# Down products of a mixture-of-experts encoder step in column tiles of 64, 32 and 32

## The chip, the cores and the metric

The kernel runs on one core of a Trainium2 chip. The metric is the device time of one execution in microseconds (us). It is given as the median of several runs of the same program.

## The reference, cut to what matters

The program is one inference step of a two-layer encoder over 256 prompt rows and 32 sample rows, 2048 features wide. Each layer ends in a hierarchical mixture of experts: a router picks one of 4 groups for each row and 2 of the 4 experts in it.

```python
hu = jnp.einsum('td,edf->tef', xt, w_gate_up)      # 2048 -> 1024, for each expert
hg, hv = jnp.split(hu, 2, axis=-1)
act = jax.nn.silu(hg) * hv * gates[..., None]      # 512 wide
out = jnp.einsum('tef,efd->td', act, w_down)       # 512 -> 2048, summed over experts
x = layer_norm(DEEPNORM_ALPHA * x + out, ln_g[i, 1], ln_b[i, 1])
```

The last product is the one that the change touches. All weights are fp32, and each layer has 16 experts of 12 MB each, so the two layers read 403 MB of expert weights.

## The kernel before, in words

Each layer works through its rows in windows, one for each group of experts (further ones would follow if a group overflowed; here there are four windows in each layer). A window holds up to `W = 96` rows ("slots") of one group, and each of its `NE = 4` experts takes up to `ES = 64` of them.

The weights of a window come as 24 chunks of 2 MB through a ring of `NSLOT = 6` slots: 4 chunks of gate and up weights ("gu") and 2 chunks of down weights ("dn") for each expert. SyncE issues them in one order (`WINDOW_ORDER`): gu0, gu1, dn0, gu2, dn1, gu3, dn2, dn3. It waits before each one until TensorE has used up the chunk that was in the slot. TensorE counts that in `parts_used`: a chunk has four parts of 1024 columns, and each part adds one.

A gu part (L1010) is two matmuls of 128 rows by 64 columns of stationary data, one at column tile 0 and one at column tile 64, with 512 moving columns each. They write partitions 0 to 63 and 64 to 127 of one PSUM bank. ScalarE and VectorE make the activations from it (L724, L725, L1522, L1523). TensorE then spreads an expert's 64 rows over the 96 slots of the window (`turn_act`, L969: 64 rows by 128 columns of the array), and ScalarE copies that to `act` (L727).

A dn part (L1023) is two matmuls with 96 slots as the stationary columns and 512 of the 2048 output columns as the moving data. A chunk has two blocks of 128 features (`f`), and each has two parts: the even part writes banks 2 and 3, the odd part banks 4 and 5. The sums of all four experts stay in these four banks over the whole window.

From the third part of dn2's second half on, each part is preceded by a pair of matmuls that picks the rows of the next window (`select_rows`, L944: 96 rows by 128 columns). ScalarE and VectorE take turns to copy them out (L700, L1439).

At the end of a window VectorE adds the four banks to the kept rows (`add_rows`, L1450). It takes the first two banks after the last but one part and the others after the last. Then come the statistics (L1454), a square root by ScalarE (`spread`, L705) and the normalisation. TensorE's first dn part of the next window waits on `z_done` until the four banks are added.

An fp32 matmul of this kernel has two records in the trace, each with its LDWEIGHTS. So L1023 has 1024 records for 512 matmuls, and L1010 has 2048 for 1024.

Of the kernel before, what the change touches and what calls it, by code (L numbers as in the profile page):

```python
# [23 lines left out]
ALU = mybir.AluOpType  # L24
ACT = mybir.ActivationFunctionType
AX = mybir.AxisListType

D = 2048
# [9 lines left out]
NG, NE = 4, 4  # L38
FE = 512
KF = FE // 128  # L40
# [40 lines left out]
OVER_AT = 3  # L81
PLACES_AT = 24
NV = 2 + 2 * NE
OUT_STEP = (16, 32)


# [3 lines left out]
def parts_base(l):  # L90

    return PARTS_LRU + PARTS_OUT + l * NG * PARTS_WIN
# [40 lines left out]
def encoder_step(nc, A, O):  # L133
    ctx = ExitStack()
    with ctx:
# [3 lines left out]
        def sem(name):  # L139
            return ctx.enter_context(nc.semaphore(name))  # L140
# [97 lines left out]
        slot_f = carve(work, 2772, 2, WINS)  # L238
        members = carve(work, 2788, 3, NG + NG * NE)
        rslot = carve(work, 2848, NE)  # L240
        Gh = members[:, :, 0:NG]
        th = carve(arena, 0, FE)
        P = carve(arena, FE, 3, WINS * W)
# [64 lines left out]
        gated = [sem(f"gated{i}") for i in two]  # L308
        sel_ready = [sem(f"sel_ready{i}") for i in two]
        act_ready = [sem(f"act_ready{i}") for i in two]  # L310
        vmoe = [sem(f"vmoe{i}") for i in two]
        x_out = [sem(f"x_out{i}") for i in two]
        P_ready = [sem(f"P_ready{i}") for i in two]
# [42 lines left out]
        def ring_at(n):  # L356
            return ring[:, slot_of(n), :]
# [165 lines left out]
        def _(eng):  # L523
# [140 lines left out]
            def moe(l):  # L664
                if l == 0:
                    eng.wait_ge(brow_in, 64)
                eng.wait_ge(lgT_done[l], 1)
                eng.activation(lgT[:, :], ps[0:20, 1, 0:T], ACT.Identity, bias=brow[:, l:l + 1]).then_inc(lgT_ready[l], 1)

                def rows(i):  # L670
                    t0, m = TILES[i]
                    evacuate_x(1 + l, False, range(4 * i, 4 * i + 4))
                    eng.wait_ge(tr_act[1 + l], 4 * i + 4)
                    eng.dma_start(x_rows[l][t0:t0 + m, :], xtok[0:m, i, :]).then_inc(x_out[l], 16)

                rows(0)
                eng.wait_ge(ex_in[l], 1)
                eng.activation(r4[1][:, :, :], r4[0][:, :, :], ACT.Exp).then_inc(ex_out[l], 1)
                rows(1)
                rows(2)  # L680
                eng.wait_ge(ex_in[l], 2)
                eng.activation(r1[3][:, :, :], r1[2][:, :, :], ACT.Exp).then_inc(ex_out[l], 1)
                if l == 0:

                    eng.wait_ge(cstT_full, 1)
                    eng.activation(cstT[:, :], ps[:, 2, 0:128], ACT.Copy).then_inc(cstT_ready, 1)
                    eng.wait_ge(cstT_ready, 1)
                    dst = [O["lru_conv_prompt"][0, 0, k] for k in range(3)] + [O["lru_conv_sample"][0, 0, k] for k in range(3)]
                    dst += [O["lru_h_prompt"][0, 0], O["lru_h_sample"][0, 0]]
                    for j, o in enumerate(dst):  # L690
                        eng.dma_start(o.rearrange("(b p) -> b p", p=128), cstT[j:128:8, :]).then_inc(out_st, 16)
                else:
                    for i, name in enumerate(("ln_g", "ln_b")):
                        eng.dma_start(ln_row[i], A[name][1, 1:2, :].to_broadcast([W, D])).then_inc(ln_row_in, 16)
                base = C_MOE0 if l == 0 else C_MOE1

                def even_rows(w, q):

                    eng.wait_ge(rows_turned[l], w * PAIRS + (q + 1))
                    eng.activation(xsel[:, 2 * q:2 * q + 2, :], ps[:, 6, :].rearrange("p (k c) -> p k c", k=2), ACT.Copy)\  # L700
                       .then_inc(xsel_even[l], 1)

                def spread(done):
                    eng.wait_ge(zvar_ready[l], done)
                    eng.activation(zr[0:W, :], zr[0:W, :], ACT.Sqrt).then_inc(zstd_ready[l], 1)  # L705

                def normalise(done, done_sem):
                    if l == 0:
                        eng.wait_ge(znorm_ready[l], done)
                        eng.activation(ZS, ZS, ACT.Identity, scale=zr[0:W, :], bias=zn[0:W, :]).then_inc(done_sem, 1)  # L710

                def window(w, first=False):
                    seq = w if l == 0 else w + act_extra[0]

                    parts0 = parts_base(l) + NPART
                    if not first:
                        spread(w)
                        normalise(w, rows_ready[l])
                    eng.wait_ge(act_turned[l], w * (NE + 1) + 1)
                    eng.activation(spread_to[0:ES, :, :], ps[0:ES, 7, 0:NE * W].rearrange("p (e s) -> p e s", e=NE),  # L720
                                   ACT.Copy).then_inc(act_ready[l], 1)
                    for e in range(NE):
                        eng.wait_ge(parts_used, seq * PARTS_WIN + (parts0 + GU_END[e]))
                        eng.activation(th[0:ES, :], ps[0:ES, e % 2, :], ACT.Tanh, scale=0.5)  # L724
                        eng.activation(up[0:ES, :], ps[ES:2 * ES, e % 2, :], ACT.Copy).then_inc(th_ready[l], 1)  # L725
                        eng.wait_ge(act_turned[l], w * (NE + 1) + (e + 2))
                        eng.activation(act[:, e % 2, :], ps[:, 6 + e % 2, 0:KF * W], ACT.Copy).then_inc(act_ready[l], 1)  # L727
                        if e == 1:
                            if not first:
                                eng.wait_ge(rows_out[l], w * OUT_STEP[l])  # L730
                            eng.activation(ZS, XS, ACT.Copy, scale=ALPHA).then_inc(kept[l], 1)
                    for q in range(0, PAIRS, 2):
                        even_rows(w + 1, q)

                for q in range(0, PAIRS, 2):
                    even_rows(0, q)
                for w in range(FLAT):
                    window(w, w == 0)
                eng.wait_ge(route_ready[l], 1)
                n_win = eng.value_load(route_i[0:1, l, 0:1], min_val=NG, max_val=NG + MORE)  # L740
                with eng.Fori(FLAT, n_win) as w:
                    window(w)
                spread(n_win)
                normalise(n_win, rows_last[l])
                if l == 0:
                    act_extra.append(eng.snap(n_win - NG))
                    eng.wait_ge(rows_out[0], eng.snap(n_win * 16))
                    eng.wait_ge(rows_turned[0], eng.snap(n_win * PAIRS + PAIRS))
                    for i, (t0, m) in enumerate(TILES):
                        eng.dma_start(xtok[0:m, i, :], n_rows[t0:t0 + m, :]).then_inc(back_in, 16)  # L750
                    for k in range(0, KD, 2):
                        eng.wait_ge(back_turned, k + 1)
                        g, b = (V_LNG + 1) * KD + k, (V_LNB + 1) * KD + k
                        eng.activation(xT[:, k, :], ps[:, k % 8, 0:T], ACT.Identity, scale=prmT[:, g:g + 1],
                                       bias=prmT[:, b:b + 1]).then_inc(x_ready[1], 1)
# [21 lines left out]
        def _(eng):  # L777
# [122 lines left out]
            def moe(l):  # L900
# [56 lines left out]
                def window(w, first=False):  # L957
# [15 lines left out]
                    for i, (kind, e, q) in enumerate(WINDOW_PARTS):  # L973
# [39 lines left out]
                        else:  # L1013
# [3 lines left out]
                            if e == 0 and q == 0:  # L1017
                                if first:
                                    eng.wait_ge(vgate[l], 2)
                                else:  # L1020
                                    eng.wait_ge(z_done[l], w * 4 + 4)
                            for half in range(2):
                                last = mm(ps[0:W, 2 + 2 * (q % 2) + half, :], act[:, e % 2, f * W:(f + 1) * W],  # L1023
                                          wt[:, half * 512:(half + 1) * 512], start=(e == 0 and f == 0),
                                          stop=(e == NE - 1 and f == KF - 1))
                        last.then_inc(parts_used, 1)

                for w in range(FLAT):
# [55 lines left out]
        def _(eng):  # L1084
# [205 lines left out]
            def moe(l):  # L1290
# [154 lines left out]
                    TT_(sel[0:W, :, :], iota_f[0:W, 0:ES].unsqueeze(1).to_broadcast([W, NE, ES]),  # L1445
                        rslot[0:W, :].unsqueeze(2).to_broadcast([W, NE, ES]), ALU.is_equal).then_inc(sel_ready[l], 1)

                def add_rows(b):
                    zb = ZS[:, b * 512:(b + 1) * 512]
                    TT_(zb, zb, ps[0:W, 2 + b, :], ALU.add).then_inc(z_done[l], 1)  # L1450

                def row_stats(done, b):
                    eng.wait_ge(z_done[l], done * 4 + (b + 1))
# [29 lines left out]
                def window(w, first=False):  # L1483
# [19 lines left out]
                    else:  # L1503
                        fetch_from(w + 1)
                        eng.wait_ge(kept[l], w + 1)
                        for b in range(4):
                            if b % 2 == 0:
                                eng.wait_ge(parts_used, seq * PARTS_WIN + (parts_base(l) + NPART + (-1 if b == 0 else 0)))
                            add_rows(b)
                        for b in range(4):  # L1510
                            row_stats(w, b)
                        row_var(w)
# [50 lines left out]
                for b in range(4):  # L1563
                    if b % 2 == 0:
                        eng.wait_ge(parts_used, eng.snap((n_win + extra) * PARTS_WIN + (parts_base(l) + NPART - (b == 0))))
                    add_rows(b)
                    row_stats(n_win, b)
                row_var(n_win)
                row_scale(n_win)
# [82 lines left out]
```

## Time and profile before

| | us |
|---|---|
| median of 3 runs (lowest to highest) | 1631.03 (1627.22 to 1642.02) |
| the profiled execution | 1641.09 |
| its span | 1639.3 |
| TensorE busy with matmuls | 1533.7 |
| VectorE busy | 498.0 |
| ScalarE busy | 366.4 |

The span runs from the first to the last instruction of the profiled execution. The mean granted TensorE clock in it was 0.962 of full speed. Busy times of different engines overlap.

### The profile page before, as it was taken

The page shows a single profiled execution, that of the slowest core. Times are in us where ns is not written, and L with a number is a line of the kernel's source. Part 1 is how long each engine was busy: PE and PEld are TensorE (multiplying, and loading weights), DVE is VectorE, ACT ScalarE, POOL GpSimd, SP SyncE. Part 2 cuts the span into 40 slices and gives each one's busy share as a digit, 9 for nine tenths or more (in the row PEclk, how much of TensorE's full clock was granted, in tenths as well). Part 3 has the DMA queues.
Part 4 walks back from the last instruction along what each step waited for, and adds up shares of the span by engine and source line. Part 5 has one row for each costly group of instructions (what it writes and reads, how often), then busy time and mean ns, then how long its engine had stood idle before and what let it go on. Part 6 is the DMA issues. An engine that isn't in the chain of part 4 may idle for free.

```text
span 1639.3 us, 16481 instructions
## 1 busy us (share of the span) xinstructions
PE 1533.7 (94%) x6944; PEld 881.7 (54%) x6944; DVE 498.0 (30%) x1046; ACT 366.4 (22%) x554; POOL 22.1 (1%) x34
## 2 busy tenths in 40 slices
PE   4999997999899999999999968979999999999995
PEld 4999996997643433443443435654344344344333
DVE  4676767554430020020020027533003003003003
ACT  3556566333300021021021011230101101101100
POOL 0000000000000000000000000000000000000000
PEclk8999998999889999999999987978999999999998
DMA  9445554542289989999999962337998999999990
GB/s 301 141 158 166 167 167 156 182 176 103 79 344 396 406 351 395 428 412 401 428 412 403 420 233 82 130 116 315 392 426 332 395 428 401 396 428 406 404 408 16
DMA packets 89045, 487.77 MB, mean 298 GB/s; under 512 B 5324, under 2 KB 59276, under 8 KB 61356
## 3 DMA queue, kind: packets, MB, share of 16 engines
q1 hardware_dynamic: 83984, 463.75, 71.6%
q0 software_dynamic: 2464, 13.37, 2.7%
q10 hardware_dynamic: 2522, 9.59, 1.8%
q8 instruction: 55, 0.90, 0.2%
q14 instruction: 20, 0.16, 0.0%
HBM read 476.15 MB, written 14.47 MB: 299 GB/s over the span
## 4 chain that ended last, share of the span: by engine, by line
PE 75%; DMA 18%; DVE 4%; ACT 1%; issue 1%; ACTq 0%; DVEq 0%; POOL 0%; POOLq 0%
PE ps L1023 22%; PE ps L1010 18%; DMA ring<-in_moe_w_down 15%; PE ps L944 5%; PE ps L840 4%; PE ps L842 4%; PE ps L841 4%; PE ps L870 2%; PE ps L872 2%; PE ps L871 2%; PE ps L1073 2%; PE ps L852 2%; PE ps L969 1%; DMA xtok<-x_rows,src_now 1%; PE ps L878 1%
## 5 line engine op out<-in xcount | busy, mean ns | idle before, releaser
L1023 PE MATMUL ps<-ring,work 128*96 128x512 f32 x1024 | 461.6, 596 | 8.1 <-DMA ring<-in_moe_w_down 8.1
L1010 PE MATMUL ps<-ring,xsel 128*64 128x512 f32 x2048 | 457.3, 602 | 1.5 <-DMA ring<-in_moe_w_gate_up 1.4
L1010 PEld LDWEIGHTS ps<-ring,xsel 128*64 128x64 f32 x2048 | 144.3, 138 | 293.7 <-issue 285.9
L1023 PEld LDWEIGHTS ps<-ring,work 128*96 128x96 f32 x1024 | 164.2, 164 | 247.0 <-issue 228.8
L1522 DVE SCALAR_TENSOR_TENSOR arena<-arena,ps 64x512 f32<-64x512 f32 x32 | 21.7, 679 | 604.5 <-ACT work L725 604.5
L840 PE MATMUL ps<-operands,whi 128*128 128x288 f32 x512 | 154.5, 302 | 9.1 <-ACT mark L597 9.1
L842 PE MATMUL ps<-operands,ring_lo 128*128 128x288 f32 x512 | 152.4, 298 | 0.0
L841 PE MATMUL ps<-ring_lo,whi 128*128 128x288 f32 x512 | 151.7, 296 | 0.0
L1153 DVE TENSOR_TENSOR ring_lo<-ring,whi 128x1024 fp32r<-128x1024 f32 x96 | 116.1, 1223 | 80.0 <-ACT whi L586 79.7
L586 ACT ACTIVATE whi<-ring 128x1024 fp32r<-128x1024 f32 x96 | 100.9, 1058 | 156.6 <-PE ps L842 97.5
L944 PEld LDWEIGHTS ps<-work,xtok 96*128 96x128 f32 x320 | 87.2, 319 | 39.9 <-issue 17.0
L724 ACT ACTIVATE arena<-ps 64x512 f32<-64x512 f32 x32 | 18.9, 590 | 396.2 <-PE ps L1010 396.1
L1439 DVE COPY xsel<-ps 128x512 f32<-128x512 f32 x40 | 27.7, 691 | 248.4 <-PE ps L944 248.4
L840 PEld LDWEIGHTS ps<-operands,whi 128*128 128x128 f32 x512 | 97.1, 190 | 9.6 <-issue 9.2
L944 PE MATMUL ps<-work,xtok 96*128 96x256 f32 x320 | 90.1, 414 | 11.6 <-DMA xtok<-x_rows,src_now 11.6
L841 PEld LDWEIGHTS ps<-ring_lo,whi 128*128 128x128 f32 x512 | 97.0, 189 | 0.4
L842 PEld LDWEIGHTS ps<-operands,ring_lo 128*128 128x128 f32 x512 | 97.0, 189 | 0.0
L870 PE MATMUL ps<-operands,whi 128*128 128x288 f32 x256 | 76.9, 300 | 12.2 <-DVE ylo L1247 12.2
L872 PE MATMUL ps<-operands,ring_lo 128*128 128x288 f32 x256 | 76.4, 298 | 0.0
L871 PE MATMUL ps<-ylo,whi 128*128 128x288 f32 x256 | 76.1, 297 | 0.0
L700 ACT ACTIVATE xsel<-ps 128x512 f32<-128x512 f32 x40 | 23.9, 597 | 181.2 <-PE ps L944 181.2
L727 ACT ACTIVATE work<-ps 128x384 f32<-128x384 f32 x32 | 15.7, 490 | 205.7 <-PE ps L969 205.7
(295 smaller groups left out, 1179.3 us busy)
## 6 DMA issues: line engine op xcount, KB each, us to landing
ring<-in_moe_w_gate_up SPq DMA_DIRECT2D x128, 2048.0 KB, 16.3
ring<-in_moe_w_down SPq DMA_DIRECT2D x64, 2048.0 KB, 19.0
ring<-in_lru_w_in SPq DMA_DIRECT2D x16, 2048.0 KB, 9.6
ring<-in_lru_w_out SPq DMA_DIRECT2D x8, 2048.0 KB, 8.8
x_rows<-xtok ACTq DMA_DIRECT2D x4, 1024.0 KB, 3.9
ring<-in_pool_w SPq DMA_DIRECT2D x4, 1024.0 KB, 18.3
xtok<-in_x_prompt SPq DMA_DIRECT2D x2, 1024.0 KB, 9.0
ring<-in_lru_w_a SPq DMA_DIRECT2D x8, 256.0 KB, 5.4
```

What stands on the lines that cost most here:

```text
L586: eng.activation(whi[:, p % NPART, :], ring_at(n)[:, at * PART:(at + 1) * PART], ACT.Copy)\
L840: mm(o, hi, yhi[:, k, :], start=(k == 0), stop=False)
L841: mm(o, hi, xlo_block(k), start=False, stop=False)
L842: last = mm(o, lo, yhi[:, k, :], start=False, stop=(k == KD - 1))
L852: last = mm(ps[:, 4 + 2 * a + b, 0:TG], wv[:, a, k, b * 128:(b + 1) * 128], UC[:, k, :], start=(k == 0), stop=(k == 1))
L870: mm(o, hi, yhi[:, k, :], start=(k == 0), stop=False)
L871: mm(o, hi, ylo[:, k, :], start=False, stop=False)
L872: last = mm(o, lo, yhi[:, k, :], start=False, stop=(k == KD - 1))
L944: last = mm(ps[:, 6 + q % 2, b * 256:(b + 1) * 256], XS.rearrange("s (c p j) -> s c j p", c=4, j=4)[:, k // 4, k % 4, :], sel[0:W, :, :].r ...
L1010: last = mm(ps[half * ES:(half + 1) * ES, e % 2, :], xsel[:, k, e * ES:(e + 1) * ES], wt[:, half * 512:(half + 1) * 512], start=(k == 0), ...
L1023: last = mm(ps[0:W, 2 + 2 * (q % 2) + half, :], act[:, e % 2, f * W:(f + 1) * W], wt[:, half * 512:(half + 1) * 512], start=(e == 0 and f ...
L1153: TT_(lo_at(n, at), ring_at(n)[:, at * PART:(at + 1) * PART], whi[:, p % NPART, :].bitcast(F32), ALU.subtract).then_inc(lo_ready, 1)
```

## The change

Each group of two full-width dn products per part becomes column-tiled products over three banks. Bank 2+r (r = 0, 1, 2) gets three matmuls that have different columns of the array: slots 0 to 63 of output block r in column tile 0 (64 wide), slots 64 to 95 of block r in the tile at column 64 (32 wide), and 32 slots of output block 3 in the tile at column 96 (32 wide). Which 32 slots of block 3 a bank holds is given by `LAST_OF_BANK`. The even part does banks 2 and 3, the odd part bank 4, and bank 5 isn't used. ScalarE copies block 3 from partitions 96 to 127 of the three banks to `last_block` in three copies, and VectorE adds block 3 from there, after a wait on `last_ready`.

```diff
+QB = 32
+LAST_OF_BANK = (2, 0, 1)
...
+                def take_last():
+
+                    for r, c in enumerate(LAST_OF_BANK):
+                        last = eng.activation(last_block[c * QB:(c + 1) * QB, :], ps[3 * QB:4 * QB, 2 + r, :], ACT.Copy)
+                    last.then_inc(last_ready[l], 1)
+
...
                     if not first:
+                        eng.wait_ge(parts_used, seq * PARTS_WIN + parts0)
+                        take_last()
                         spread(w)
                         normalise(w, rows_ready[l])
...
+                extra = 0 if l == 0 else act_extra[0]
+                eng.wait_ge(parts_used, eng.snap((n_win + extra) * PARTS_WIN + (parts_base(l) + NPART)))
+                take_last()
                 spread(n_win)
                 normalise(n_win, rows_last[l])
...
-                            for half in range(2):
-                                last = mm(ps[0:W, 2 + 2 * (q % 2) + half, :], act[:, e % 2, f * W:(f + 1) * W],
-                                          wt[:, half * 512:(half + 1) * 512], start=(e == 0 and f == 0),
-                                          stop=(e == NE - 1 and f == KF - 1))
+                            wt = ring_at(n)[:, (f % 2) * D:(f % 2 + 1) * D]
+                            start, stop = e == 0 and f == 0, e == NE - 1 and f == KF - 1
+                            for r in ((0, 1), (2,))[q % 2]:
+                                c = LAST_OF_BANK[r]
+                                for rows, slots0, d in ((0, 0, r), (2 * QB, 2 * QB, r), (3 * QB, c * QB, 3)):
+                                    m = 2 * QB if rows == 0 else QB
+                                    last = mm(ps[rows:rows + m, 2 + r, :], act[:, e % 2, f * W + slots0:f * W + slots0 + m],
+                                              wt[:, d * 512:(d + 1) * 512], start=start, stop=stop, tile_position=(0, rows))
                         last.then_inc(parts_used, 1)
...
-                def add_rows(b):
+                def add_rows(b, done):
                     zb = ZS[:, b * 512:(b + 1) * 512]
-                    TT_(zb, zb, ps[0:W, 2 + b, :], ALU.add).then_inc(z_done[l], 1)
+                    if b == 3:
+                        eng.wait_ge(last_ready[l], done)
+                    TT_(zb, zb, ps[0:W, 2 + b, :] if b < 3 else last_block[0:W, :], ALU.add).then_inc(z_done[l], 1)
```

## Rows read from the trace of the kernel before

**Rows 1.** The page: busy time by engine, and the clock and DMA in 40 slices.

```profile
PE 1533.7 (94%) x6944; PEld 881.7 (54%) x6944; DVE 498.0 (30%) x1046; ACT 366.4 (22%) x554; POOL 22.1 (1%) x34
...
PEclk8999998999889999999999987978999999999998
DMA  9445554542289989999999962337998999999990
```

**Rows 2.** The page's costliest groups: busy us, mean ns of one, idle before.

```profile
L1023 PE MATMUL ps<-ring,work 128*96 128x512 f32 x1024 | 461.6, 596 | 8.1 <-DMA ring<-in_moe_w_down 8.1
L1010 PE MATMUL ps<-ring,xsel 128*64 128x512 f32 x2048 | 457.3, 602 | 1.5 <-DMA ring<-in_moe_w_gate_up 1.4
```

**Rows 3.** Two windows behind the first, layer 0: busy by engine, PEclk, DMA share, GB/s.

```profile
598.65:724.20 125.55, 124.08 (x455) 50.66 (x456) 14.99 (x31) 16.22 (x22) 1.84 (x2) 1.00 1.00 412
724.20:849.77 125.57, 124.22 (x455) 50.65 (x456) 15.15 (x31) 16.22 (x22) 1.84 (x2) 1.00 1.00 414
```

**Rows 4.** DMA issues: count, KB each, median us to landing.

```profile
ring<-in_moe_w_gate_up SPq DMA_DIRECT2D x128, 2048.0 KB, 16.3
ring<-in_moe_w_down SPq DMA_DIRECT2D x64, 2048.0 KB, 19.0
```

**Rows 5.** The timeline of TensorE's matmuls in window 1, layer 0: start, us, what.

```profile
604.99 8.80 PE L1010 MATMUL ps<-ring,xsel 128*64 128x512 f32 x40
613.73 7.11 PE L1023 MATMUL ps<-ring,work 128*96 128x512 f32 x16
620.77 1.18 PE L969 MATMUL ps<-work,arena 64*128 64x96 f32 x8
621.87 7.11 PE L1023 MATMUL ps<-ring,work 128*96 128x512 f32 x16
628.91 14.02 PE L1010 MATMUL ps<-ring,xsel 128*64 128x512 f32 x64
```

**Rows 6.** The timeline of weight loads there: start, us, what, idle before.

```profile
598.58 0.20 PEld L1010 LDWEIGHTS ps<-ring,xsel 128*64 128x64 f32 x4
...
599.07 0.14 PEld L1010 LDWEIGHTS ps<-ring,xsel 128*64 128x64 f32 x2 [0.29 <-issue]
599.50 0.14 PEld L1010 LDWEIGHTS ps<-ring,xsel 128*64 128x64 f32 x2 [0.29 <-issue]
...
619.39 0.16 PEld L1023 LDWEIGHTS ps<-ring,work 128*96 128x96 f32 x1 [0.27 <-issue]
619.82 0.16 PEld L1023 LDWEIGHTS ps<-ring,work 128*96 128x96 f32 x1 [0.27 <-issue]
620.76 1.01 PEld L969 LDWEIGHTS ps<-work,arena 64*128 64x128 f32 x8 [0.78 <-issue]
```

**Rows 7.** The line L1010 by itself: ns min/median/max of a record.

```profile
L1010 PE MATMUL ps<-ring,xsel x2048: 592/592/1112, 448.1 to 1582.8; 128*64 128x512 f32 x187
```

**Rows 8.** The timeline of matmuls where the next window's rows are picked.

```profile
681.69 3.67 PE L1023 MATMUL ps<-ring,work 128*96 128x512 f32 x8
685.21 1.08 PE L944 MATMUL ps<-work,xtok 96*128 96x256 f32 x4
686.12 1.88 PE L1023 MATMUL ps<-ring,work 128*96 128x512 f32 x4
687.84 1.08 PE L944 MATMUL ps<-work,xtok 96*128 96x256 f32 x4
```

**Rows 9.** Stretches late in the first window of layer 0; columns as in rows 3.

```profile
570.00:575.00 5.00, 5.00 (x16) 3.08 (x16) 0.69 (x1) 0.60 (x1) 0.00 (x0) 1.00 0.41 170
575.00:580.00 5.00, 5.00 (x17) 3.29 (x16) 0.77 (x2) 1.88 (x2) 0.00 (x0) 1.00 0.70 223
580.00:585.00 5.00, 5.00 (x15) 1.68 (x15) 2.41 (x6) 0.00 (x0) 0.00 (x0) 1.00 0.48 200
585.00:590.00 5.00, 5.00 (x26) 1.70 (x24) 3.80 (x12) 1.05 (x2) 0.00 (x0) 1.00 0.93 326
```

**Rows 10.** The last window of layer 1: its last dn chunks, and the final adds.

```profile
1584.51 7.10 PE L1023 MATMUL ps<-ring,work 128*96 128x512 f32 x16 [1.07 <-DMA ring<-in_moe_w_down]
...
1615.51 5.31 PE L1023 MATMUL ps<-ring,work 128*96 128x512 f32 x12
...
1619.14 0.68 DVE L1450 TENSOR_TENSOR xtok<-xtok,ps 96x512 f32<-96x512 f32 x1 [2.63 <-PE ps L1023]
...
1623.10 0.67 DVE L1450 TENSOR_TENSOR xtok<-xtok,ps 96x512 f32<-96x512 f32 x1
```

**Rows 11.** ScalarE's copy of 64 partitions by 512 columns out of PSUM.

```profile
L725 ACT ACTIVATE work<-ps 64x512 f32<-64x512 f32 x32 | 19.0, 593 | 0.4
```

More of the change, by code:

```diff
@@ L240, in encoder_step @@
         rslot = carve(work, 2848, NE)
+        last_block = carve(work, 3584, 512)
         Gh = members[:, :, 0:NG]
@@ L310, in encoder_step @@
         act_ready = [sem(f"act_ready{i}") for i in two]
+        last_ready = [sem(f"last_ready{i}") for i in two]
         vmoe = [sem(f"vmoe{i}") for i in two]
@@ L1508, in window @@
                                 eng.wait_ge(parts_used, seq * PARTS_WIN + (parts_base(l) + NPART + (-1 if b == 0 else 0)))
-                            add_rows(b)
+                            add_rows(b, w)
                         for b in range(4):
@@ L1565, in moe @@
                         eng.wait_ge(parts_used, eng.snap((n_win + extra) * PARTS_WIN + (parts_base(l) + NPART - (b == 0))))
-                    add_rows(b)
+                    add_rows(b, n_win)
                     row_stats(n_win, b)
```

## The prediction

> **What bounds the kernel now.** I read the busy times first [rows 1]: TensorE is busy for 94% of the span, and in the slices of the expert windows (11 to 22 and 27 to 38) both it and the DMA engines stand at 8 or 9 tenths. The costliest groups [rows 2] are the two products of the experts: 461.6 us of down products (L1023) and 457.3 us of gate and up products (L1010). The windows view by window [rows 3] decides what a saving on TensorE can be worth. A window takes 125.6 us, TensorE is busy for 124.1 to 124.2 of them, and the DMA share is 1.00 at 412 to 414 GB/s. So the two are level. The issues view says the same: a chunk of 2 MB lands 16 to 19 us after its issue [rows 4], while 24 chunks in 125.6 us are one in 5.2 us. Some three chunks are thus always queued. TensorE waits for the ring only 9.5 us in all [rows 2] because it is just about as slow as the loads. VectorE and ScalarE are idle for over two thirds of the span.
>
> **How matmuls follow each other.** The change stands or falls with this, so I read the timeline for it. In a run of equal shapes a new record starts every 0.43 us: the weight loads of L1023 stand 0.43 us apart [rows 6], and 16 records end 7.11 us after the first starts [rows 5], which is 15 x 0.43 plus the 0.59 of the last one. In the gate and up products the loads come in pairs every 0.43 us [rows 6], and 40 records take 8.80 us [rows 5], which is 19 x 0.43 + 0.59 with some slack. So two tiles of 64 columns run at the same time, and equal tiles are known to be concurrent here.
>
> Where the shape of the tile changes it is different. L1010's 40 records begin at 604.99 and end at 613.79, and L1023 begins at 613.73, with the records' length of 0.59 [rows 5, 7] and not their spacing of 0.43 between the last start and the next. The 16 records of L1023 end at 620.84, and L969 (64 rows by 128 columns) begins at 620.77; those of the next chunk end at 628.98, and L1010 begins at 628.91 [rows 5]. The weight load in front isn't started early either: 0.78 us pass without a load, against 0.27 inside a run [rows 6]. Each of these changes of tile shape thus lets the array run empty. The two that I can compare cost 0.59 - 0.43 = 0.16 us, and then the first spacing is 0.49 (598.58 to 599.07 [rows 6]) in place of 0.43.
>
> The Trainium skill says of this (TensorEngine Tiling (Array Packing), section Tiling Modes) that changing the tiling mode, and not just the tile, drains TensorE, and it lists 128x64 and 128x32 as different modes. The rows above agree with the drain for 64 against 128 columns; none shows 64 beside 32.
>
> **The change part by part.**
>
> *The products.* Before, a block f has 4 matmuls, that is 8 records; a chunk has two blocks, 16 records, and takes 7.04 us (613.73 to 620.77 [rows 5]). After, a block has 3 banks with 3 matmuls each, 18 records. No row shows a 64-column tile beside 32-column ones, so the cost of a bank has two ends.
> - Lower end: all three tiles run together as the pairs of L1010 do. A bank takes 2 x 0.43 = 0.86 us and a chunk 6 x 0.86 = 5.15. That is 1.9 us less than now, or 1.7 without the drain at the end of the chunk.
> - Upper end: the 64-column tile and each 32-column tile drain each other. A tile alone takes 0.49 + 0.59 = 1.08 us, a bank 3.24, a chunk 19.4.
> - Between them: 64 and 32 columns are different shapes, but the two 32-column tiles are equal and run together. A bank takes 1.08 for the first and 1.08 for the pair, 2.16 us, and a chunk 6 x 2.16 = 12.96 us.
>
> I take the third. The rows that are nearest to a change from 64 to 32 columns are the changes from 64 to 128 and from 128 by 128 to 64 by 128, and each of them drained, also where the new tile begins at the same corner as the old. Then a chunk costs 12.96 - 7.04 = 5.92 us more, and 64 chunks 379 us.
>
> *What TensorE no longer waits for.* At 24 x 5.2 us the loads are far ahead of a window that takes 170 us, so the ring waits of 9.5 us go [rows 2].
>
> *The picks of the next rows.* A pick and a part take 2.63 us together (685.21 to 687.84) and a part 1.72 (686.12 to 687.84), so a pick is 0.91 us now, with no drain since both are 128 wide [rows 8]. After, it follows and precedes other shapes: it keeps its last record's full 0.40 (1.08 us for four records less three spacings of 0.22) in place of 0.22, and the first spacing grows by 0.06. That is about 0.2 us for each of 64, or 13 us.
>
> *ScalarE's three copies.* Each moves 32 by 512; the nearest row is 64 by 512 at 0.59 us [rows 11], so 1.8 us after a window's last part. They are hidden: VectorE's adds and statistics of blocks 0 to 2 fill some 4 us, as now (1619.14 to 1623.10 [rows 10]), before it wants block 3. Queued behind the new wait on ScalarE are `spread` and `normalise`, which need VectorE's later results anyway, and then the copy for the next window's activations, some 14 us of TensorE work away. I take nothing. Without that cover it would be 1.8 us at each of the two layer ends.
>
> *The last adds.* The final part is one bank. VectorE starts on blocks 0 and 1 that long before the end (2.16 us against 1.7), and its work of eight steps ends about when it did. In the lower case the bank is 0.86 us, and each layer ends 0.9 us later against TensorE.
>
> *Sum.* 379 - 9.5 + 13 = +382 us on the profiled execution of 1641, so 2023. The median of the runs shown stands 10 us below that execution, which gives 2013.
>
> **The rivals.**
>
> *A. All three tiles run together: faster.* For it speaks that tiles of different columns do run together in L1010, and that every drain in the rows is between shapes that overlap in the array, which 64, 32 and 32 don't. TensorE's window would fall by 8 chunks x 1.7 = 14 us to 110. But the loads fill all of 125.6 us in the windows behind the first [rows 3], so there the 14 us become ring waits. What is left is the time in which the DMA engines are idle now: in the first window of a layer their share is 0.41, 0.70, 0.48 and 0.93 between 570 and 590 [rows 9], which is 7.4 us idle, and I take as much for layer 1. And the end of a layer: the last ring wait is before dn2, at 1584.5 [rows 10], and the four chunks behind it save 4 x 1.7 = 6.9 us. That is 14.3 us for a layer, 29 for both, less 2 for the later adds; a few us may come from packing the loads tighter. 27 to 36 us less gives 1641 - 30 = 1611, and 1601 against the median.
>
> *B. The tiles run together only in part: slower by a little.* If records start in the program's order and the second record of a tile holds back the next tile, three tiles need three spacings, 1.29 us for a bank and 3.86 for a block, against 3.43 now. That is 0.43 x 16 = 6.9 us more in a window, of which 1.5 are today's wait: +5.4 x 8 = 43 us, 1675. Against it speaks that the pairs of L1010 start together from their first record on (four loads within 0.20 us, and 2 for each spacing [rows 6]).
>
> *C. All three drain each other.* By the upper end a chunk costs 12.4 us more, +790, so 2430.
>
> The other side of my forecast is A. It decides at the cost of a bank: below 4/3 x 0.86 = 1.14 us the change saves TensorE time, and above it the kernel is slower, since the loads leave only 1.5 us in a window.
>
> **How the numbers follow.** Drain between 64 and 32: 0.54. A: 0.36, of which 0.03 fall within 1%, since the loads could leave less than I count. B: 0.06. C: 0.04. So faster by over 1% is 0.33, within 1% is 0.03, slower is 0.64; 1% is about what a measurement of this kernel can tell from no change. The likeliest case is the drain, 2013 us. Its own range comes from the spacing after a drain (0.43 or 0.51 in place of 0.49) and the picks: 1965 to 2045. The range has to reach A at 1590 to leave out no more than 2 in 10, and takes in B; it ends at 2050.
>
> **What would show each step.** Drain: L1023's busy time rises from 461.6 to about 830 us, the records stand 0.4 to 0.6 us apart one by one in the 64-column tile and in pairs behind it, the ring waits vanish, the DMA share in a window drops from 1.00 to about 0.75, and a window takes 170 us. A: three records start within some ns of each other every 0.43 us, L1023 is busy about 345 us, and TensorE gets waits on the down and gate loads of over 10 us a window at a DMA share of 1.00. B: a chunk takes 7.7 us. ScalarE's copies are right if no wait of VectorE on them is longer than a few tenths. The prediction is wrong if the array takes tiles of unequal width at the same time; everything else in the sum is small beside that.

## The result, and the profile after

The changed kernel takes 1955.5 us (median of 4 runs, 1946.1 to 1958.4) against 1633.1 for the kernel before. The ratio is 1.196, with a 95% interval from 1.193 to 1.200. The profiled execution has a span of 1956.6 us, 317 us more than before.

The page of the changed kernel, its busy times, clock and DMA in 40 slices, to be read against [rows 1]:

```profile
PE 1861.6 (95%) x8224; PEld 849.3 (43%) x8224; DVE 498.6 (25%) x1046; ACT 380.4 (19%) x578; POOL 22.1 (1%) x34
...
PEclk8999989998999999999999969899999999999998
DMA  8555554426883985896598234387769839858930
```

TensorE is as busy as ever, at 95%, but the DMA row has lost most of its nines in the expert windows. VectorE's 498.6 us are those of before, and ScalarE has 14 us more for 24 copies. So whatever grew is on TensorE. The groups of the changed kernel with different shapes kept apart (busy us, mean ns of one):

```profile
L1025 PE MATMUL ps<-ring,xsel 128*64 128x512 f32 x2048 | 455.1, 600 | 0.0
L1043 PE MATMUL ps<-ring,work 128*64 128x512 f32 x768 | 410.5, 616 | 0.0
L1043 PE MATMUL ps<-ring,work 128*32 128x512 f32 x1536 | 404.0, 605 | 0.0
```

The down products are now L1043. They took 461.6 us [rows 2]; now their 64-column tiles alone are busy for 410.5 us and the 32-column tiles for 404.0. If the two kinds ran side by side these two numbers would be the same stretch of time. The page has 768.8 us for both together. That is 45.7 less than their sum of 814.5, or 0.06 for each of the 768 turns of a width. That is about how far the row of a turn's last matmul runs on past the start of the next shape, and no overlap of the work. The ring waits behind both products are gone.

The weight loads in the changed kernel's window 1, layer 0, show the pattern (start us, us, what, idle before):

```profile
657.42 0.14 PEld L1043 LDWEIGHTS ps<-ring,work 128*32 128x32 f32 x4 [0.81 <-issue]
658.41 0.19 PEld L1043 LDWEIGHTS ps<-ring,work 128*64 128x64 f32 x2 [0.84 <-issue]
659.41 0.14 PEld L1043 LDWEIGHTS ps<-ring,work 128*32 128x32 f32 x4 [0.81 <-issue]
660.39 0.19 PEld L1043 LDWEIGHTS ps<-ring,work 128*64 128x64 f32 x2 [0.84 <-issue]
```

Two loads of 64 columns, then four of 32, then two of 64, each group about a microsecond after the other, with 0.81 to 0.84 us in which nothing is loaded. That gap is the mark of a change of tile shape that [rows 6] had too (0.78, against 0.27 to 0.29 inside a run). The tile of 64 columns has the array to itself for 1.00 us (658.41 to 659.41), then the two of 32 have it for 0.98 (659.41 to 660.39). A bank takes 1.98 us.

The timeline of the same stretch gives the chunk, and a stretch of layer 1's last window gives the picks; both in the changed kernel:

```profile
656.47 11.93 PE L1043 MATMUL ps<-ring,work 128*64 128x512 f32 x36
668.33 1.18 PE L984 MATMUL ps<-work,arena 64*128 64x96 f32 x8
669.44 11.98 PE L1043 MATMUL ps<-ring,work 128*64 128x512 f32 x36
681.35 9.23 PE L1025 MATMUL ps<-ring,xsel 128*64 128x512 f32 x42
...
1907.04 1.30 PE L959 MATMUL ps<-work,xtok 96*128 96x256 f32 x4
1908.27 4.04 PE L1043 MATMUL ps<-ring,work 128*64 128x512 f32 x12
```

A chunk takes 11.86 to 11.91 us (656.47 to 668.33, 669.44 to 681.35) where it took 7.04 [rows 5], and a pick 1.23 (1907.04 to 1908.27) where it took 0.91 [rows 8]. That accounts for the result: 64 x 4.85 = 310 us, 64 x 0.32 = 21, less the ring waits of 9.5, is 321 us, beside the 317 by which the span grew.

Two windows of the changed kernel (busy by engine, clock, DMA share, GB/s), and the times from issue to landing:

```profile
641.43:806.72 165.29, 165.29 (x614) 46.71 (x613) 15.09 (x31) 17.99 (x25) 1.84 (x2) 1.00 0.79 315
806.72:972.01 165.29, 165.29 (x613) 46.70 (x613) 15.24 (x31) 17.99 (x25) 1.84 (x2) 1.00 0.78 314
...
ring<-in_moe_w_gate_up SPq DMA_DIRECT2D x128, 2048.0 KB, 12.1
ring<-in_moe_w_down SPq DMA_DIRECT2D x64, 2048.0 KB, 10.6
```

A window is 165.3 us instead of 125.6 [rows 3]. TensorE has no idle time in it, and the loads use 0.79 of the DMA engines and land after 11 to 12 us instead of 16 to 19 [rows 4]: the two are no longer level.

### The profile page after: what moved, and what is told of

The parts are those of the page before. It is cut to its first block, busy times and chain, and to the rows that moved or that the text cites. A ratio compares the mean times of both kernels' runs of the same rounds, so it can differ in the third digit from the quotient of the medians.

```text
span 1956.6 us, 19069 instructions
## 1 busy us (share of the span) xinstructions
PE 1861.6 (95%) x8224; PEld 849.3 (43%) x8224; DVE 498.6 (25%) x1046; ACT 380.4 (19%) x578; POOL 22.1 (1%) x34
## 4 chain that ended last, share of the span: by engine, by line
PE 92%; DVE 3%; DMA 2%; ACT 1%; issue 1%; ACTq 0%; DVEq 0%; POOL 0%; POOLq 0%
PE ps L1043 39%; PE ps L1025 23%; PE ps L959 5%; PE ps L855 4%; PE ps L857 4%; PE ps L856 3%; PE ps L984 2%; PE ps L885 2%; PE ps L887 2%; PE ps L886 2%; PE ps L1092 2%; PE ps L867 1%; DMA xtok<-x_rows,src_now 1%; PE ps L893 1%; PE ps L1066 1%
## 5 line engine op out<-in xcount | busy, mean ns | idle before, releaser
L1043 PE MATMUL ps<-ring,work 128*32 128x512 f32 (+1 forms) x2304 | 768.8, 608 | 0.0
L1043 PEld LDWEIGHTS ps<-ring,work 128*32 128x32 f32 (+1 forms) x2304 | 130.6, 117 | 570.4 <-issue 568.1
L959 PE MATMUL ps<-work,xtok 96*128 96x256 f32 x320 | 104.9, 460 | 12.3 <-DMA xtok<-x_rows,src_now 12.3
L959 PEld LDWEIGHTS ps<-work,xtok 96*128 96x128 f32 x320 | 82.5, 325 | 69.7 <-issue 53.7
## 6 DMA issues: line engine op xcount, KB each, us to landing
ring<-in_moe_w_gate_up SPq DMA_DIRECT2D x128, 2048.0 KB, 12.1
```

The costliest lines, as they stand in the source:

```text
L959: last = mm(ps[:, 6 + q % 2, b * 256:(b + 1) * 256], XS.rearrange("s (c p j) -> s c j p", c=4, j=4)[:, k // 4, k % 4, :], sel[0:W, :, :].r ...
L1043: last = mm(ps[rows:rows + m, 2 + r, :], act[:, e % 2, f * W + slots0:f * W + slots0 + m], wt[:, d * 512:(d + 1) * 512], start=start, stop ...
```

## The experiments

Theory W: a change between 64 and 32 columns empties the array, and equal tiles run together however many they are. Rival N: the array runs at most two of these fp32 tiles at a time, whatever their widths.

**Four tiles of 32** (e1_four_of_32). Nothing but the widths is changed.

```diff
-for rows, slots0, d in ((0, 0, r), (2 * QB, 2 * QB, r), (3 * QB, c * QB, 3)):
-    m = 2 * QB if rows == 0 else QB
+for rows, slots0, d in ((0, 0, r), (QB, QB, r), (2 * QB, 2 * QB, r), (3 * QB, c * QB, 3)):
+    m = QB
```

Expected: 

> All down products in four column tiles of 32: slots 0 to 31, 32 to 63 and 64 to 95 of block r, and block 3 at column 96; everything else as in the changed kernel. Theory W (a change between 64 and 32 columns empties the array; equal tiles run together however many they are): a bank takes 2 x 0.43 = 0.86 us instead of 1.98, a chunk 5.15 us, the loads become the bound, and the time is about 1600 us (1590 to 1615). Rival N (the array runs at most two of these fp32 tiles at a time, whatever their widths): a bank takes at least 4 x 0.43 = 1.72 us, a chunk 10.3, and the time is about 1633 + 64 x 3.3 = 1840 us.

Measured: 1606.5 us, 0.985 of the kernel before (0.980 to 0.989). That is 349 us less than the changed kernel, with a third more matmuls in the down products. The weight loads of this kernel, in the same place of the window:

```profile
601.24 0.16 PEld L1043 LDWEIGHTS ps<-ring,work 128*32 128x32 f32 x8 [0.81 <-issue]
601.70 0.13 PEld L1043 LDWEIGHTS ps<-ring,work 128*32 128x32 f32 x4 [0.30 <-issue]
602.12 0.13 PEld L1043 LDWEIGHTS ps<-ring,work 128*32 128x32 f32 x4 [0.30 <-issue]
602.55 0.13 PEld L1043 LDWEIGHTS ps<-ring,work 128*32 128x32 f32 x4 [0.30 <-issue]
```

Four loads every 0.43 us: four tiles run at once, and the only long gap is the one in front, where the 64-column tiles of the gate and up products end. N is out. This version is faster than the kernel before too, by 1.5%.

**Widths grouped** (e2_widths_grouped). The same matmuls as in the changed kernel, in an order with fewer changes.

```diff
-for r in ((0, 1), (2,))[q % 2]:
-    for rows, slots0, d in ((0, 0, r), (2 * QB, 2 * QB, r), (3 * QB, c * QB, 3)):
+banks = ((0, 1), (2,))[q % 2]
+wide = [(r, 0, 0, r) for r in banks]
+narrow = [t for r in banks for t in ((r, 2 * QB, 2 * QB, r), (r, 3 * QB, LAST_OF_BANK[r] * QB, 3))]
+for r, rows, slots0, d in wide + narrow:
```

Expected: 

> The changed kernel with the even part's matmuls in another order: first the 64-column tiles of banks 2 and 3, then the four 32-column tiles of both; two changes of width in that part instead of four. Theory W: the four records of 64 columns take 0.48 + 0.43 + 0.43 + 0.52 = 1.86 us and the four pairs of 32 columns 1.84, together 3.70 us against 3.97 now; 0.27 us for each of 128 even parts are 35 us, so about 1920 us. Rival N (at most two tiles at a time, no matter the widths): the order changes nothing that the width did, about 1955 us.

Measured: 1921.0 us, 1.176 of before (1.172 to 1.180). The median is 34.5 us below the changed kernel's and the span of the profiled execution, 1917.9 us, is 38.7 below. There are 256 changes of width less, so one costs 0.13 to 0.15 us. The rest of the loss stays, since the 64-column tiles still have the array alone. The weight loads of an even part show it:

```profile
653.22 0.19 PEld L1044 LDWEIGHTS ps<-ring,work 128*64 128x64 f32 x2 [0.84 <-issue]
...
655.08 0.14 PEld L1044 LDWEIGHTS ps<-ring,work 128*32 128x32 f32 x4 [0.81 <-issue]
...
656.92 0.19 PEld L1044 LDWEIGHTS ps<-ring,work 128*64 128x64 f32 x2 [0.84 <-issue]
```

The two 64-column tiles take 1.86 us one after the other (653.22 to 655.08), and the four of 32 columns, in pairs, 1.84 (655.08 to 656.92).

**Without the fourth tile, and with a second tile of 64** (e3_no_fourth_tile, e6_two_of_64). Each leaves part of the down products out or misplaced. The two differ in the width of one tile (the first keeps the fourth tile for one of a window's 16 blocks).

```diff
 # e3
+    if rows == 3 * QB and not start:
+        continue
-    ... start=start, stop=stop, tile_position=(0, rows))
+    ... start=start, stop=stop or rows == 3 * QB, tile_position=(0, rows))
 # e6
-for rows, slots0, d in ((0, 0, r), (2 * QB, 2 * QB, r), (3 * QB, c * QB, 3)):
-    m = 2 * QB if rows == 0 else QB
+for rows, slots0, d in ((0, 0, r), (2 * QB, QB, r)):
+    m = 2 * QB
```

Expected of the first: 

> The changed kernel with the tile at column 96 issued only for the first block of a window, so that output block 3 misses the other 15 blocks; what runs is one tile of 64 columns and one of 32 for each bank. Theory W: the two still take turns, a bank stays at 1.98 us, and the time is within 1% of 1956 us. Rival N: two tiles run together, a bank takes 0.86 us, and the time falls to about 1600 us.

Expected of the second: 

> As the run without the fourth tile, but the second tile is 64 columns wide as well: slots 32 to 95 at column 64, so that rows 64 to 95 hold other slots' sums and block 3 is no product. Only the width of the second tile differs from that run, and three banks are used. Theory W: equal widths run together, 0.86 us for a bank and about 1600 us. Rival N gives the same here. A third reading, that a second tile in the down products waits for another reason (the part's counting, the order of the two records of a matmul), gives about 1950 us.

Measured: 1953.0 and 1610.4 us, one execution each. The shapes of the down products in the first run (two rows), then in the second (one row):

```profile
L1045 PE MATMUL ps<-ring,work 128*64 128x512 f32 x768 | 410.5, 616 | 0.0
L1045 PE MATMUL ps<-ring,work 128*32 128x512 f32 x816 | 401.6, 605 | 0.0
```

```profile
L1043 PE MATMUL ps<-ring,work 128*64 128x512 f32 x1536 | 353.6, 599 | 11.3 <-DMA ring<-in_moe_w_down 11.3
```

With nearly half of the 32-column matmuls left out (816 records in place of 1536), those tiles are still busy for 401.6 us, since a tile of 32 columns by itself takes as long as two. Two tiles are enough for the loss, and 32 more columns in one of them take it away. It is the width, not the number of tiles, the column at which they begin, or the order of a matmul's two records. No run puts 32 columns into a tile of 64, so a tile's width and the number of columns it uses are not told apart for these two. For full-width tiles [rows 8] tell them apart: products with 96 stationary columns and picks with 128 follow each other there at the full pace of 0.43 us.

**Three blocks at full width** (e4_three_blocks_wide). No tiles at all; this asks what a saving of a quarter of the down products is worth.

```diff
-for half in range(2):
+for half in range(2 if q % 2 == 0 or (e == 0 and f == 0) else 1):
...
-    ... stop=(e == NE - 1 and f == KF - 1))
+    ... stop=(e == NE - 1 and f == KF - 1) or (q % 2 == 1 and half == 1))
```

Expected: 

> The kernel before, but the fourth output block (bank 5) is multiplied only for the first of a window's 16 blocks of features, so that 15 of its 16 contributions are missing. TensorE's down work falls to three quarters with no tiles and no changes of width at all. Reading 'the loads are the bound' (rival A's account): the windows behind the first stay near 124.5 us with ring waits of 6 to 8 us each, and only the first windows and the ends of the layers get shorter; 1595 to 1612 us, as with four tiles of 32. Rival reading (four tiles of 32 lose something of their own, above all in the changes of shape around the picked rows): this run is clearly faster than four tiles of 32, 1575 to 1590 us.

Measured: 1601.5 us, 0.979 of before (0.977 to 0.982). So four tiles of 32 give up little against nearly the same saving without tiles: 5 us by the medians, and 9 by the ratios of 0.985 and 0.979, which were taken on different chips. Where TensorE waits in this run, then in the one with four tiles of 32 (us in total, times, longest):

```profile
PE ps L1010 <- DMA ring<-in_moe_w_gate_up: 44.2, 22, 5.3
PE ps L1023 <- DMA ring<-in_moe_w_down: 17.8, 17, 1.4
```

```profile
PE ps L1025 <- DMA ring<-in_moe_w_gate_up: 37.0, 19, 5.6
PE ps L1043 <- DMA ring<-in_moe_w_down: 10.2, 9, 1.3
```

In this run the down products are busy for 103 us less (358.5 in place of 461.6). Of that, 52 us come back as waits for the weights (62.0 in place of 9.5) and 13 in slower gate and up products (470.3 in place of 457.3); the span is 38 us shorter. With four tiles of 32 it is 109 us less (352.8), of which 38 come back as waits, 12 in the gate and up products and 12 in the picks (102.2 in place of 90.1); the span is 37 us shorter, and about 10 are not accounted for by these rows.

So the reading that four tiles of 32 lose something of their own around the picked rows is true in part. In the first window of layer 0 of that run, eight picks and the seven parts between them take 20.3 us (547.91 to 568.19), and 19.3 in the kernel before (559.66 to 579.00): there the tiles save nothing. The window takes 124.2 us with four tiles of 32 (447.60 to 571.76) and 121.6 in this run (448.52 to 570.09). In the windows behind it the weights are waited for either way.

**Half of the down loads** (e7_four_of_32_half_dn_loads, e8_before_half_dn_loads), on four tiles of 32 and on the kernel before.

```diff
+if kind == "dn":
+    src, dst = src[:, 0:SLOT // 2], dst[:, 0:SLOT // 2]
```

The second half of each down chunk then holds older data.

Expected of the first: 

> The run with four tiles of 32, with only the first half of each down chunk loaded, so that the second half holds older data; the same instructions otherwise. The loads of a window fall from 24 chunks to 20. If the loads are what bounds that run, its ring waits (47 us in all) go for the most part and the time falls by 35 to 50 us, to about 1560 us. If something on TensorE or the copies behind it bounds it, the time stays within 1% of 1606 us.

Expected of the second: 

> The kernel before with only the first half of each down chunk loaded, so that the second half holds older data. TensorE is level with the loads there: its ring waits are 9.5 us. Theory: those waits go and nothing else changes, 1618 to 1626 us. Rival (loads and products also slow each other down, by memory traffic or by late slots): 1600 us or less.

Measured: 1543.6 and 1624.3 us, one execution each. So the loads do bound the version with four tiles of 32; it gains more than I expected, 60 us of span (1602.3 to 1541.9). Its waits of 47 us explain the larger part. The rest is in the gate and up products, which are busy for 469.6 us with the waits and 455.9 without them. The reason is the clock. Four stretches of 5 us of the version with four tiles of 32, around its ring wait of 3.2 us (columns as in [rows 3]):

```profile
618.00:623.00 5.00, 2.01 (x10) 0.43 (x6) 0.00 (x0) 0.00 (x0) 0.00 (x0) 0.93 0.99 298
623.00:628.00 5.00, 4.77 (x12) 1.49 (x14) 0.00 (x0) 0.00 (x0) 0.00 (x0) 0.50 1.01 429
628.00:633.00 5.00, 5.00 (x22) 1.36 (x18) 0.00 (x0) 0.00 (x0) 0.00 (x0) 0.89 1.02 436
633.00:638.00 5.00, 5.00 (x50) 1.46 (x48) 1.36 (x2) 1.19 (x2) 0.00 (x0) 1.00 1.02 436
```

After the stretch in which TensorE was busy for 2.01 of 5 us, the granted clock is 0.50 for the next one, that is 1.2 instead of 2.4 GHz, and the products run at half their pace until it is back. The timeline of TensorE there shows what it costs, and that it doesn't follow every wait:

```profile
623.23 10.01 PE L1025 MATMUL ps<-ring,xsel 128*64 128x512 f32 x32 [3.21 <-DMA ring<-in_moe_w_gate_up]
...
644.85 7.09 PE L1025 MATMUL ps<-ring,xsel 128*64 128x512 f32 x32
...
657.38 3.65 PE L1025 MATMUL ps<-ring,xsel 128*64 128x512 f32 x16 [1.25 <-DMA ring<-in_moe_w_gate_up]
```

Behind the wait of 3.21 us, 32 records take 10.01 us in place of 7.09; behind one of 1.25 us, 16 records take the usual 3.65. The whole run has five ring waits of 3.2 to 5.6 us. The 32 records behind them take 10.01, 8.78, 10.01, 8.80 and 9.94 us, 12.1 us more than five times 7.09, which is nearly all of the 13.7. The other ring waits, of 2.2 us at most, are followed by records at the usual pace. A long ring wait is thus dearer than its own length, and a short one isn't.

On the kernel before, 1624.3 us lies in the range that I gave for the case that only its waits go. It is 10 us under the median of 1634.5 measured beside it, and the waits are 9.5. (Against the span of the profiled execution it is 17, but that execution was 8 us above its median.)

**The copies alone** (e5_copies_alone). The full-width products of before, with block 3 taken out of bank 5 by ScalarE.

```diff
-last = eng.activation(last_block[c * QB:(c + 1) * QB, :], ps[3 * QB:4 * QB, 2 + r, :], ACT.Copy)
+last = eng.activation(last_block[c * QB:(c + 1) * QB, :], ps[c * QB:(c + 1) * QB, 5, :], ACT.Copy)
```

Expected: 

> The products of the kernel before (96 slots, four banks) with the change's other half: ScalarE copies output block 3 out of bank 5 in three copies of 32 partitions, and VectorE adds it from there after the wait on ScalarE. Theory: the copies are hidden behind VectorE's first adds, no change, within 0.3% of before. Rival: the copies and the load of the square root's table behind them lie on the path at the end of each window, at least 1.8 us at each layer's end, and the next window's activations wait too: 1637 to 1650 us.

Measured: 1634.8 us, 1.000 of before (0.998 to 1.001). The copies cost nothing that can be measured.

**Pairs of 64, then four of 32** (e9_pairs_of_64_then_32s). A forecast from theory W: both widths may be used if they take few turns and each fills the array. All products are made, but some lie where the adds don't look for them.

```diff
-for r in ((0, 1), (2,))[q % 2]:
-    for rows, slots0, d in ((0, 0, r), (2 * QB, 2 * QB, r), (3 * QB, c * QB, 3)):
+if q % 2 == 0:
+    tiles = [(b, half * ES, ES, 0, 2 * b + half) for b in range(2) for half in range(2)]
+else:
+    tiles = [(2, c * QB, QB, 2 * QB, c) for c in range(4)]
+for r, rows, m, slots0, d in tiles:
```

Expected: 

> Both widths in use, but never side by side: the even part multiplies slots 0 to 63 of all four output blocks as two pairs of 64-column tiles (banks 2 and 3), the odd part slots 64 to 95 of the four blocks as four 32-column tiles in bank 4. All products are made, but lie where the adds that follow don't look for them, so the sums that reach the rows are mixed up. Two changes of width for each block of features, against six in the changed kernel. Theory W (the price is one of each change, about 0.15 us, and of what a lone tile leaves unused): the even part takes 0.48 + 0.43 + 0.43 + 0.52 = 1.86 us, the odd part 0.45 + 0.53 = 0.98, a chunk 5.7 us; that is 0.4 us more than four tiles of 32 and under the loads' pace, so 1604 to 1614 us, faster than before. Rival (mixing widths costs by itself, whatever the order): a chunk of over 8 us and a time above 1660 us.

Measured: 1610.0 us, 0.987 of before (0.985 to 0.990). A chunk (32 records) in its timeline, with the loads of its first block:

```profile
601.87 5.75 PE L1044 MATMUL ps<-ring,work 128*64 128x512 f32 x32
607.55 1.18 PE L984 MATMUL ps<-work,arena 64*128 64x96 f32 x8
```

```profile
603.68 0.16 PEld L1044 LDWEIGHTS ps<-ring,work 128*32 128x32 f32 x8 [0.81 <-issue]
604.68 0.20 PEld L1044 LDWEIGHTS ps<-ring,work 128*64 128x64 f32 x4 [0.84 <-issue]
```

A chunk takes 5.68 us (601.87 to 607.55), where I had 5.7, and the turn of the 32-column tiles 1.00 (603.68 to 604.68), where I had 0.98. Changes of width by themselves are bearable, at two for each block of features.

## Why the prediction came out as it did

**The step on which it stood was right.** I took tiles of 64 and 32 columns to drain each other and the two of 32 to run together. The loads of the changed kernel show that order, and the runs with equal widths show that width is the reason. The turns of 1.00 and 0.98 us show that the rule cited from the Trainium skill (TensorEngine Tiling (Array Packing), section Tiling Modes) holds here also for tiles side by side that share no column of the array, which no row of before could show. Rival C is excluded by the four loads that start together; N and rival B by the four tiles of 32.

**One term was mis-sized: the bank.** I had 1.08 + 1.08 = 2.16 us, and it took 1.00 + 0.98 = 1.98. The last record of a run holds the next shape back for some 0.52 us from its start, not for the 0.59 that its row is long. The rows of before held this already. The 40 records of [rows 5] have one spacing of 0.49 at their start, as the run of [rows 6] has, so the last of them starts at 604.99 + 0.49 + 18 x 0.43 = 613.2, and the next shape follows at 613.73. I counted 19 equal spacings and took the row's end for the end of the work. A chunk was 11.9 us, not 12.96, which is 69 us less over 64 chunks. My sum was +382 us and the span grew by 317, which is 65 less: 69 less for the bank and 8 more for the picks make 61, and 4 are left open. In the medians it is 2013 against the measured 1955.5. My own range for the drain, 1965 to 2045, started 10 us too high.

**The picks** cost 0.32 us more each, 21 us in all against my 13. I had counted a change of shape on both sides, but with the wrong sizes. Inside the four records of a pick 0.22 us are added (its row is 1.30 us long at 1907.04, and 1.08 in [rows 8]), where I had 0.06, and 0.10 behind its last record, where I had 0.18.

**The ring waits** went, as predicted, and the DMA share in a window fell to 0.79 (I had 0.75, for a window of 170 us; it was 165.3).

**ScalarE's copies** were worth nothing, as predicted, but my reason holds at the layer ends only. There VectorE's statistics stand between the adds, and it didn't wait for the copies. In the other windows the four adds follow each other at once, and VectorE did wait for the copies. In the changed kernel `add_rows` is L1471, and its waits for ScalarE are in this row, 6.9 us over six windows, up to 1.1 at a time:

```profile
DVE xtok L1471 <- ACT work L710: 6.9, 6, 1.1
```

I had called a wait of more than a few tenths a sign against me, and by that sign the reason was wrong. The time doesn't show it: the run with the copies alone has the same waits (6.8 us over six windows) and is no slower.

**Rival A's premise was wrong for these widths; its total was close, in part by luck.** With four equal tiles its mechanism comes true: 1606.5 us measured against my 1601. In the windows behind the first the gain on TensorE mostly turns into waits for the loads, as argued, but TensorE is busy for 117 and 116 us there, and not for 110, since the picks and the slower clock take some back. The terms were off both ways. The first window of a layer is 11.9 us shorter (from 136.1 to 124.2, in both layers), where I had 7.4 (1.7 of the 11.9 are a lower clock at the start of the window in the execution of before, 52 records in 13.08 us against 11.38); the three windows behind it together are 3.9 and 4.6 us shorter, where I had 6.9.

**Slips in the working**, none of which moves the forecast by more than 2 us: 15 x 0.43 + 0.59 is 7.04, and the 7.11 of the row has the first spacing of 0.49 in it; 0.18 + 0.06 for a pick is 0.24, or 15 us in all; the 2430 of rival C stands against the profiled execution, and is 2420 against the median.

## What to carry to other kernels

When packing the columns of the array, choose one tile width for a run of products and let several tiles of it fill the array. A narrow tile beside a wider one is not a filler: the two widths take turns. Where two widths are needed, let each fill the array and change between them as seldom as possible; a change cost 0.13 to 0.15 us here, and two for each block of features were hardly felt (1610.0 us against 1606.5). The runs show this for fp32 products with 512 moving columns over all 128 rows. Before that, look at what the saving can be worth: on a kernel whose loads are level with TensorE, a quarter off the largest product was worth 2%, with waits and a lower clock in place of most of the rest.

## What the runs showed that I had not expected

A ring wait of 3.2 us was followed by 5 us at a granted clock of 0.50; over the run with four tiles of 32, five such waits came to 12 us beside 47 us of waits. That tiles of 32 and 64 columns drain each other although they lie in different columns I had expected at 0.54, hardly more than even; [rows 6] had shown only that equal tiles run together. And four fp32 tiles of 32 columns keep the spacing of 0.43 us of a single tile, with 48 records in a chunk of 5.3 us.
